# Five of eight row blocks of the mixer's output projection computed inside the attention steps, with VectorE's scaling of probabilities moved ahead of the next row maxima

## The chip, the cores and the metric

One NeuronCore of a Trainium2 chip runs the whole program: a two-layer decoder step in fp32, for one prompt of 512 tokens and 8 samples of 4 new tokens, 544 tokens in all. The metric is the device time of one execution in microseconds, the median of several runs.

## The reference

Each layer is a gated feed-forward block, a token mixer, a second feed-forward block and a small gated embedding. The change lies in the mixer, whose three branches are normalised apart, joined and projected:

```python
def _token_mixing(u, w, cache):
    z = u @ w['w_in']
    qa, ka, va, xb, gb, qc, kc, vc, oc, ic, fc = jnp.split(z, SPLIT_IDX, axis=-1)
    ...
    ya = _rms(_combine(parts).reshape(B, T, D_A).astype(u.dtype), w['g_out_a'])
    hb, hT, new_buf = _rglru(xb, conv_buf, h0, w)
    yb = _rms(jax.nn.gelu(gb) * hb.astype(u.dtype), w['g_out_b'])
    ...
    hc = jax.nn.sigmoid(oc).reshape(B, T, N_HEADS_C, DV_C) * hc.astype(u.dtype)
    yc = _rms(hc, w['g_out_c'].reshape(N_HEADS_C, DV_C)).reshape(B, T, D_C)
    y = jnp.concatenate([ya, yb, yc], axis=-1) @ w['w_out']
```

Branch A is dilated attention (384 features, 6 heads), branch B a gated linear recurrence (384), branch C a matrix memory (256). `w_out` is 1024 by 1024, so in blocks of 128 it has 8 row blocks: 3 for A, 3 for B, 2 for C.

## The kernel before

Activations lie feature-major, 128 features by 544 tokens to a tile, in two halves of 272 tokens. A precise fp32 product is made of three matmuls in the type fp32r: `block3` (L468, matmul on L473) multiplies high part by high part, high by low and low by high, for each half, so one 128 x 128 weight block costs 6 matmuls of 272 columns. Weights come in chunks of 8 blocks (512 KB). SyncE loads a chunk into one of two `raw` buffers (L392), ScalarE casts it to the high part `wh` (L922, `split`), GpSimd subtracts to get the low part `wl` (L1689, `lo_parts`), and TensorE uses it; `wh` and `wl` are rings of four chunks. A load waits until the chunk two before it has its low part (`lo`), a cast until the chunk four before it has been used (`used`). Every engine runs its own program in the order in which it is written; semaphores are the only ties.

The mixer of one layer runs in this order. First 24 tiles of the input projection, of which the last six stand between the steps of branch C's memory (`spread_g`, `qk`, `read`, `update` on TensorE, t = 0 to 3, L701), after branch B is done. Then `STEPS_A` = 15 attention steps (L828). There are 12 pairs, a pair being two heads and one block of 128 queries, with 128, 256, 384 or 512 keys by turns. In step i TensorE issues `scores(i)`, `values(i-2)` and `turn(i-1)` (transposes of the probabilities, L738), and after them, in certain steps, work for the samples against the cache: `sample_scores`, `sample_turn`, `sample_values`, `sample_out`. VectorE finds the row maxima of pair i (L1544) as soon as its scores are there, then scales the probabilities of pair i-1 by the inverse of their sums (`by_sum`, L1550), then copies the output of pair i-2 (L1599), then does its sample work. ScalarE computes the exponentials of pair i (L1088) and copies the transposed probabilities of pair i-1 out of PSUM (L1099). Scores take PSUM banks 0 and 1, the samples 2 and 3, transposes 4 and 5, and values 6 and 7 by turns. SyncE loads the key and value cache in eight groups (m = 0 to 7) of four 672 KB loads into two halves, each when TensorE has freed its half (`kv_used`). The chunks of the output projection wait: five were loaded before the attention, but the two masks for the samples lie in the ring slot of the fourth.

After the last step ScalarE squares all 8 branch tiles (L1127), TensorE sums them over the partitions (L862), ScalarE turns the four means into inverse roots (L1131, L1133), and VectorE and ScalarE make the high and low parts of the 8 normalised tiles (L1327, L1167, L1322). Only then does the output projection start: eight output tiles of 8 blocks each, the first three interleaved block by block. VectorE copies each finished tile out of PSUM (L1276), ScalarE squares it (L928) and VectorE sums the squares (L1224) for the norm that follows.

## Time and profile before

| | us |
|---|---|
| median of 3 runs | 2561.22 (2561.19 to 2565.79) |
| the profiled execution | 2555.39 |
| its span, from first to last instruction | 2553.7 |
| mean granted clock of TensorE, of full speed | 0.966 |
| TensorE matmul busy | 2395.2 (94% of the span) |
| VectorE, ScalarE, GpSimd busy | 975.2, 795.4, 872.3 |
| chain that ended last, on TensorE | 85% |

Busy shares are means over the whole span; the attention of layer 0 lies between 640 and 725 us and that of layer 1 between 1907 and 1992 us. In the stretches view the columns are the length, then TensorE's matmuls, its weight loads, VectorE, ScalarE and GpSimd, each with busy microseconds and instructions, then the granted clock of TensorE, the share of the DMA engines and GB/s. In groups and timelines PE is TensorE, DVE VectorE, ACT ScalarE, POOL GpSimd and SPq SyncE's DMA queue; a bracket tells how long the engine was idle before the row and what ended that.

### The profile page before, as it was taken

The numbers are of one execution on the slowest core, as the hardware profiler recorded it, in microseconds if no ns is written. First come the engines' busy times: TensorE is split into PE (matmuls) and PEld (weight loads), VectorE is DVE, ScalarE is ACT, GpSimd is POOL, SyncE is SP. The second block draws the span as 40 slices with busy tenths as digits, with TensorE's granted clock in tenths as the row PEclk, the third lists the DMA queues.
The fourth block names the chain that finished last, engine by engine and source line by source line (L and its number), as shares of the span: only waits on it lengthen the run. The fifth ranks groups of instructions, "written<-read, shape, count | busy, mean of one in ns | idle before, by whom it ended". The sixth has DMA issues, their size and how long they took to land.

```text
span 2553.7 us, 42609 instructions
## 1 busy us (share of the span) xinstructions
PE 2395.2 (94%) x18938; PEld 2298.0 (90%) x18938; DVE 975.2 (38%) x1363; ACT 795.4 (31%) x1141; POOL 872.3 (34%) x374
## 2 busy tenths in 40 slices
PE   6999999999788999999899999989997889999996
PEld 6999998988368999999889999989883789999996
DVE  3333303665445333202553331047554453332035
ACT  3222223331434322223442222234213442222243
POOL 3433443432013434344333344424210234434431
PEclk9999999999889999999999999999888999999998
DMA  3222232222812322332222222322128123222221
GB/s 125 98 90 88 91 98 84 83 81 70 312 62 66 107 90 83 100 99 90 70 72 90 87 85 91 100 68 91 65 89 317 62 67 99 82 90 100 93 90 52
DMA packets 72287, 247.40 MB, mean 97 GB/s; under 512 B 14296, under 2 KB 14560, under 8 KB 72160
## 3 DMA queue, kind: packets, MB, share of 16 engines
q1 hardware_dynamic: 72160, 245.59, 28.6%
q8 instruction: 95, 1.56, 0.2%
q14 instruction: 32, 0.26, 0.0%
HBM read 238.68 MB, written 6.88 MB: 96 GB/s over the span
## 4 chain that ended last, share of the span: by engine, by line
PE 85%; DVE 9%; ACT 4%; issue 1%; DMA 1%; SPq 0%; POOL 0%; DVEq 0%; ACTq 0%
PE psum L473 77%; PE psum L778 1%; DVE y_z L1673 1%; PE psum L738 1%; PE psum L812 1%; DVE x L1237 1%; DVE pp L1544 1%; PE psum L726 1%; PE psum L862 1%; DVE y_ff L1234 1%; ACT sq L928 1%; DVE xc L1361 1%; PE psum L603 1%; PE psum L637 1%; DVE z L1338 0%
## 5 line engine op out<-in xcount | busy, mean ns | idle before, releaser
L1689 POOL TENSOR_TENSOR wl<-raw,wh 128x1024 fp32r<-128x1024 f32 x356 | 863.9, 2428 | 1593.2 <-ACT wh L922 1593.1
L473 PE MATMUL psum<-xh,wh 128*128 128x272 f32 x4096 | 866.9, 293 | 83.2 <-DVE xl L1230 27.8
L473 PE MATMUL psum<-xh,wl 128*128 128x272 f32 x4096 | 857.2, 291 | 0.0
L473 PE MATMUL psum<-xl,wh 128*128 128x272 f32 x4096 | 855.2, 291 | 0.0
L473 PEld LDWEIGHTS psum<-xh,wh 128*128 128x128 f32 x4096 | 655.7, 192 | 93.2 <-DVE xl L1230 30.3
L922 ACT CAST wh<-raw 128x1024 fp32r<-128x1024 f32 x356 | 372.5, 1047 | 1133.5 <-PE psum L473 1066.1
L473 PEld LDWEIGHTS psum<-xl,wh 128*128 128x128 f32 x4096 | 654.9, 192 | 0.0
L473 PEld LDWEIGHTS psum<-xh,wl 128*128 128x128 f32 x4096 | 650.1, 192 | 0.0
L473 PE MATMUL psum<-hh,wl 128*128 128x272 f32 x1408 | 291.5, 288 | 0.0
L473 PE MATMUL psum<-hh,wh 128*128 128x272 f32 x1408 | 291.1, 288 | 0.0
L473 PE MATMUL psum<-hl,wh 128*128 128x272 f32 x1408 | 290.2, 288 | 0.0
L1267 DVE TENSOR_TENSOR hl<-act_out,hh 128x544 fp32r<-128x544 f32 x88 | 217.6, 2473 | 90.5 <-ACT hh L969 90.5
L1265 DVE TENSOR_TENSOR act_out<-act_out,psum 128x544 f32<-128x544 f32 x88 | 63.5, 721 | 415.8 <-PE psum L473 405.1
L473 PEld LDWEIGHTS psum<-hh,wh 128*128 128x128 f32 x1408 | 221.4, 188 | 0.0
L473 PEld LDWEIGHTS psum<-hl,wh 128*128 128x128 f32 x1408 | 221.3, 189 | 0.0
L473 PEld LDWEIGHTS psum<-hh,wl 128*128 128x128 f32 x1408 | 219.8, 189 | 0.0
L1274 DVE TENSOR_TENSOR y_ff<-psum,r 128x544 f32<-128x544 f32 x32 | 23.2, 725 | 448.5 <-PE psum L473 448.5
L1262 DVE TENSOR_TENSOR act_out<-psum,r 128x544 f32<-128x544 f32 x88 | 63.6, 723 | 182.0 <-PE psum L473 133.2
L928 ACT ACTIVATE sq<-y_ff 128x544 f32<-128x544 f32 x32 | 21.1, 659 | 157.5 <-DVE y_ff L1274 157.5
L1338 DVE TENSOR_TENSOR z<-psum,r 128x544 f32<-128x544 f32 x48 | 34.0, 719 | 93.2 <-PE psum L473 75.2
L947 ACT ACTIVATE xh<-x,pc 128x544 fp32r<-128x544 f32 x64 | 47.9, 748 | 48.3 <-DVE x L1237 48.3
L966 ACT ACTIVATE act_out<-act_out 128x544 f32<-128x544 f32 x88 | 57.5, 653 | 14.5 <-DVE act_out L1262 14.4
(218 smaller groups left out, 1485.5 us busy)
## 6 DMA issues: line engine op xcount, KB each, us to landing
raw<-in_weights SPq DMA_DIRECT2D x356, 512.0 KB, 3.5
kv<-in_kc SPq DMA_DIRECT2D x32, 672.0 KB, 7.8
kv<-in_vc SPq DMA_DIRECT2D x32, 672.0 KB, 6.5
x<-in_x SPq DMA_DIRECT2D x4, 544.0 KB, 7.1
out_x<-x SPq DMA_DIRECT2D x8, 272.0 KB, 2.0
mask<-in_consts SPq DMA_DIRECT2D x4, 456.0 KB, 3.8
out_v<-z SPq DMA_DIRECT2D x2, 816.0 KB, 4.3
out_k<-z SPq DMA_DIRECT2D x2, 816.0 KB, 4.4
```

The costliest lines, as they stand in the source:

```text
L473: ins = pe.matmul(T(t)[:, h, :], w, r[:, h, :], start=first and n == 0, stop=last and n == 2)
L603: ins = pe.matmul(psum[:, 2, h * P:h * P + n], ident[0:HC, h:h + 1].to_broadcast([HC, P]), gg[:, t * P:t * P + n], start=True, stop=True)
L637: ins = pe.matmul(psum[r, 5, o:o + n], w, at_[0:n, 2 * c + p, 0:n], start=True, stop=(t == 0))
L922: act.copy(wh[:, G % RING, :], raw[:, G % 2, :]).then_inc(hi.sem, 1)
L928: act.activation(sq[:, k % 2], src, ACT.Square).then_inc(sq_ready.sem, 1)
L947: act.activation(xh[:, k], x[:, k], ACT.Copy, scale=g).then_inc(nh_ready.sem, 1)
L966: act.activation(act_out[:, f % 2], act_out[:, f % 2], ACT.Silu).then_inc(silu_ready.sem, 1)
L1262: ve.tensor_tensor(act_out[:, b], T(2 * b), r2[:], ALU.mult).then_inc(gate_ready.sem, 1)
L1265: ve.tensor_tensor(act_out[:, b], act_out[:, b], T(2 * b + 1), ALU.mult).then_inc(h_ready.sem, 1)
L1267: ve.tensor_tensor(hl[:, f], act_out[:, b], hh[:, f].bitcast(F32), ALU.subtract) \
L1338: ve.tensor_tensor(two, T(t), r2[:], ALU.mult).then_inc(z_ready.sem, 1)
L1689: po.tensor_tensor(wl[:, G % RING, :], raw[:, G % 2, :], wh[:, G % RING, :].bitcast(F32), ALU.subtract).then_inc(lo.sem, 1)
```

## The change

The output projection is split by row blocks. The part for branches B and C (5 of 8 blocks) is cut into 16 fills, one for each output tile and half of the tokens; a fill is 15 matmuls into one PSUM bank, copied to SBUF. Twelve are issued in attention steps 3 to 14, ahead of `turn`, one right after the last step and three behind the sum of attention's squares. The part for branch A (3 blocks) follows attention, and VectorE adds it to the copied early part. For this, branch B is normalised within the memory steps and split into high and low parts; branch C in attention steps 0 to 2. The weights of one layer become 182 chunks instead of 178: eight of 5 blocks (`X_OB`), four of two times 3 blocks (`X_OA`) in place of eight of 8. SyncE loads chunks between the cache loads. The masks of the samples leave the weight ring, and values use PSUM bank 6 alone, fills bank 7. Apart from that, VectorE's scaling of pair i-1 moves ahead of the row maxima of pair i. The names `CH_...` become `X_...` throughout, which isn't shown.

```diff
@@ block.sync: between the cache loads, m = 0 to 7
-                load_to(CH_D2 + 5)
+                    if m == 1 or m >= 4:
+                        load_to(X_OB + (6 if m == 1 else m + 3))
+                load_to(X_D2 + 5)
...
@@ block.tensor: memory steps
                     qk(t + 1)
                     read(t)
                     update(t)
+                    if t == 1:
+                        pe.wait_ge(z_ready.sem, z_ready.at(L, E_MEM + 2))
+                        group_mean(T(0), ones, [z2[:, k] for k in range(ZXB, ZXB + 3)], 1)
+                        pe.wait_ge(gr_ready.sem, gr_ready.at(L, 1))
...
+                def fill(u, bank):
+                    d, h = u // 2, u % 2
+                    G = L * X_ALL + X_OB + d
+                    if u == 0:
+                        pe.wait_ge(nl_ready.sem, nl_ready.at(L, N_OUT * KT + B_BLOCKS))
+                    elif u <= FILL_END:
+                        pe.wait_ge(fill_ready.sem, fill_ready.at(L, u))
+                    if h == 0:
+                        pe.wait_ge(lo.sem, G + 1)
+                    for n, (k, l, m) in enumerate(EARLY):
+                        w_h, w_l = (v[:, G % RING, n * P:(n + 1) * P] for v in (wh, wl))
+                        for o, (w, r) in enumerate(((w_h, zr[:, m, h, :]), (w_h, zr[:, l, h, :]), (w_l, zr[:, m, h, :]))):
+                            ins = pe.matmul(psum[:, bank, 0:HALF], w, r, start=n == 0 and o == 0,
+                                            stop=n == B_BLOCKS - 1 and o == 2)
+                    ins.then_inc((used if h else fill_done).sem, 1)
...
@@ block.tensor: values
-                    if j >= 2:
-                        pe.wait_ge(o_ready.sem, o_ready.at(L, j - 1))
+                    if j:
+                        pe.wait_ge(o_ready.sem, o_ready.at(L, j))
...
-                            ins = pe.matmul(psum[r, 6 + j % 2, 0:P], vt[:, kb, h * HD:(h + 1) * HD],
+                            ins = pe.matmul(psum[r, 6, 0:P], vt[:, kb, h * HD:(h + 1) * HD],
...
@@ block.tensor: attention steps and what follows
+                    if i == 1:
+                        pe.wait_ge(tm_ready.sem, tm_ready.at(L, 11))
+                        for c, t in enumerate((T(1), T(3))):
+                            group_mean(t, blk, [z2[:, ZQC + c]], 4 + c)
+                    if i == 2:
+                        pe.wait_ge(gr_ready.sem, gr_ready.at(L, 3))
                     if 2 <= i < PAIRS + 2:
                         values(i - 2)
+                    if i >= FILL_STEP:
+                        fill(i - FILL_STEP, 7)
                     if 1 <= i < PAIRS + 1:
                         turn(i - 1)
...
+                fill(FILL_END, 7)
+                group_mean(T(0), ones, [xh_sq[:, k] for k in range(3)], 6)
+                for u in range(FILL_END + 1, 2 * KT):
+                    fill(u, 7 - (u - FILL_END))
+                pe.wait_ge(gr_ready.sem, gr_ready.at(L, 4))
...
@@ block.scalar: memory steps
+                    if t == 2:
+                        for n in range(3):
+                            early_hi(L, n)
                     split(G + E_MEM + t + RING)
+                    if t == 0:
+                        act.wait_ge(b_done.sem, b_done.at(L, 1))
+                        for k in range(3):
+                            act.activation(z2[:, ZXB + k], z2[:, ZGB + k], ACT.Square).then_inc(gs_ready.sem, 1)
+                    if t == 1:
+                        group_rstd(L, 1, acc[:], T(0), DB)
...
@@ block.scalar: ahead of and in the attention steps
+                split(G + 3)
+                act.wait_ge(c_done.sem, c_done.at(L, 1))
+                for c in range(2):
+                    act.activation(z2[:, ZQC + c], z2[:, ZVC + c], ACT.Square).then_inc(gs_ready.sem, 1)
...
+                    if i == 1:
+                        for c in range(2):
+                            group_rstd(L, 2 + c, z2[:, ZOC + c], T(1 + 2 * c), HD)
+                    if i == 2:
+                        for c in range(2):
+                            early_hi(L, 3 + c)
+                    if i >= FILL_STEP:
...
+                        act.copy(Y_OUT[d][:, h, :], psum[:, 7, 0:HALF]).then_inc(fill_ready.sem, 1)
+                        if h and d < 5:
+                            split(G + d + RING)
...
@@ block.vector: late projection
+            def out_a(L):
+                for d in range(KT):
...
+                    ve.tensor_tensor(Y_OUT[d], Y_OUT[d], T(d % 4), ALU.add).then_inc(y_ready.sem, 1)
+                    if 1 <= d < KT - 1:
+                        add_square(L, 1, d)
...
@@ block.vector: memory steps
+                    if t == 2:
+                        ve.wait_ge(gr_ready.sem, gr_ready.at(L, 1))
+                        for n in range(3):
+                            early_normed(L, n, acc[:])
+                    if t == 3:
+                        for n in range(3):
+                            early_lo(L, n)
                     z_tile(L, E_MEM + t)
...
@@ block.vector: attention steps; the same lines are taken out behind the row maxima
                 for i in range(STEPS_A):
+                    if 1 <= i < PAIRS + 1:
+                        pair = (2 * i - 2, 2 * i - 1)
+                        n = ((i - 1) % 4 + 1) * P
+                        for u in pair:
+                            ve.wait_ge(e_ready.sem, e_ready.at(L, u + 1))
+                            ve.reciprocal(stat[:, u % 4, 3:4], stat[:, u % 4, 2:3]).then_inc(ri_ready.sem, 1)
+                        for u in pair:
+                            ve.wait_ge(ri_ready.sem, ri_ready.at(L, u + 1))
+                            by_sum(stat[:, u % 4], pp[:, u % 4, 0:n]).then_inc(p_done.sem, 1)
...
+                        ve.wait_ge(gr_ready.sem, gr_ready.at(L, 3))
+                        for c in range(2):
+                            early_normed(L, 3 + c, z2[:, ZOC + c])
+                    if i == 2:
+                        for c in range(2):
+                            early_lo(L, 3 + c)
```

`early_normed` is one `scalar_tensor_tensor` on a tile, `early_hi` ScalarE's cast of it to the high part, `early_lo` VectorE's subtraction; `group_mean` is two matmuls for each tile of squares, `group_rstd` an Ln and an Exp.

## Rows read from the trace of the kernel before

**Rows 1.** Stretches view: length, then busy us (instructions) by engine, granted clock, DMA.

```profile
554.00:612.00 58.00, 57.35 (x462) 49.82 (x461) 22.13 (x41) 13.09 (x29) 16.96 (x12) 0.94 0.22 75
...
640.00:725.10 85.10, 61.72 (x574) 33.14 (x573) 37.13 (x167) 31.53 (x91) 0.00 (x0) 0.86 0.70 267
```

**Rows 2.** Chain that ended last: start us, us, what.

```profile
50.68 373.10 PE psum L473 x2976
...
738.57 50.00 PE psum L473 x384
```

**Rows 3.** Groups view, attention stretch, TensorE: busy us, mean ns | idle before.

```profile
L738 PE MATMUL psum<-con,pp 128*128 128x128 f32 x60 | 11.4, 331 | 17.4 <-DVE pp L1550 17.4
```

**Rows 4.** Timeline, TensorE, attention steps: start us, us, instructions [idle before].

```profile
648.78 0.66 PE L738 MATMUL psum<-con,pp 128*128 128x128 f32 x2 [3.40 <-DVE pp L1550]
...
652.95 1.12 PE L738 MATMUL psum<-con,pp 128*128 128x128 f32 x4 [1.31 <-DVE pp L1550]
...
654.31 3.98 PE L778 MATMUL psum<-kv,qbd 128*32 128x456 f32 x24 [0.25 <-DMA kv<-in_kc]
...
722.52 0.55 PE L825 MATMUL psum<-con,so 128*128 128x128 f32 x3 [0.68 <-DVE so L1629]
```

**Rows 5.** Chain that ended last, in the recurrent branch.

```profile
489.45 0.92 PE psum L566 x4
```

**Rows 6.** Timeline of ScalarE, attention steps and group norm.

```profile
644.50 0.83 ACT L1080 COPY vs<-psum 16x384 f32<-16x384 f32 x2
...
660.95 0.72 ACT L1088 ACTIVATE pp<-pp,stat 128x512 f32<-128x512 f32 x1 [6.47 <-DVE stat L1547]
...
668.06 0.39 ACT L1088 ACTIVATE pp<-pp,stat 128x128 f32<-128x128 f32 x1
...
669.06 1.07 ACT L1099 COPY ptp<-psum 128x512 f32<-128x512 f32 x2
...
724.29 4.48 ACT L1127 ACTIVATE y_ff<-z 128x544 f32<-128x544 f32 x8 [8.63 <-DVE z L1611]
...
730.46 0.66 ACT L1133 ACTIVATE gr<-gr 128x544 f32<-128x544 f32 x1
```

**Rows 7.** Timelines of VectorE and ScalarE, late in the output projection.

```profile
767.12 2.47 DVE L1224 TENSOR_TENSOR acc<-acc,sq 128x544 f32<-128x544 f32 x1 [1.20 <-ACT sq L928]
...
777.89 1.04 ACT L922 CAST wh<-raw 128x1024 fp32r<-128x1024 f32 x1
...
778.02 0.73 DVE L1224 TENSOR_TENSOR acc<-acc,sq 128x544 f32<-128x544 f32 x1 [0.73 <-ACT sq L928]
...
788.60 0.72 DVE L1276 COPY y_z<-psum 128x544 f32<-128x544 f32 x1 [3.84 <-PE psum L473]
```

**Rows 8.** Timeline of VectorE, attention steps.

```profile
667.77 0.88 DVE L1550 TENSOR_SCALAR pp<-pp,stat 128x512 f32<-128x512 f32 x2
...
723.11 1.10 DVE L1611 COPY z<-psum 64x16 f32<-64x16 f32 x6 [0.64 <-PE psum L825]
```

**Rows 9.** Stretches view, two pieces of the attention steps.

```profile
704.00:708.00 4.00, 2.32 (x19) 1.30 (x20) 3.08 (x12) 1.45 (x5) 0.00 (x0) 1.00 0.75 255
...
712.00:716.00 4.00, 4.00 (x32) 2.74 (x32) 0.29 (x1) 1.49 (x4) 0.00 (x0) 0.57 0.06 20
```

**Rows 10.** Timelines of VectorE and GpSimd, memory steps.

```profile
594.04 0.42 DVE L1473 TENSOR_TENSOR kw<-kc,wt 128x256 f32<-128x256 f32 x1
...
604.73 2.40 POOL L1689 TENSOR_TENSOR wl<-raw,wh 128x1024 fp32r<-128x1024 f32 x1 [8.26 <-ACT wh L922]
...
605.56 1.84 DVE L1473 TENSOR_TENSOR kw<-kc,wt 128x256 f32<-128x256 f32 x1
```

**Rows 11.** Timeline of TensorE, first matmuls of the output projection.

```profile
740.84 0.66 PE L473 MATMUL psum<-xh,wh 128*128 128x272 f32 x2
...
741.29 0.66 PE L473 MATMUL psum<-xl,wh 128*128 128x272 f32 x2
```

**Rows 12.** DMA issues: out<-in, count, KB each, us from issue to landing.

```profile
kv<-in_kc SPq DMA_DIRECT2D x32, 672.0 KB, 7.8
```

More of the change, by code:

```diff
@@ L239, in build @@
         quarters = lambda v: v.rearrange("p (q n) -> p q n", q=4)
+        Y_FF, Y_Z = ([v[:, k] for k in range(KT)] for v in (y_ff, y_z))
+        Y_OUT = [xl_y[:, k] for k in range(3)] + [z2[:, k] for k in Y_TILES]
         def column(L, c):
@@ L592, in turn_v, with group_mean @@
                     ins.then_inc(tm_done.sem, 1)
+                def group_mean(t, over, squares, first):
+                    for k, sq_k in enumerate(squares):
+                        pe.wait_ge(gs_ready.sem, gs_ready.at(L, first + k))
+                        for h in range(2):
+                            ins = pe.matmul(t[:, h, :], over, sq_k[:, h, :], start=(k == 0),
+                                            stop=(k == len(squares) - 1))
+                    ins.then_inc(gst_done.sem, 1)
                 def z_tile(e, t):
@@ L881, in _ @@
                 mix_tensor(pe, L)
-                first_tiles(L, N_OUT, G + CH_OUT)
-                for d in range(4, KT):
-                    pe.wait_ge(y_ready.sem, y_ready.at(L, KT + d - 3))
-                    tile(d % 4, G + CH_OUT + d)
+                out_a(L)
                 y_mean_square(L, 1)
```

343 lines of the change are left out of this document (207 added, 136 removed).

## The prediction

> **What bounds the kernel now.** I read the stretches view first. Between 554 and 612 us, where the last input-projection tiles run between the memory branch's steps, TensorE is busy 57.35 of 58.00 us; in layer 0's attention steps, 640 to 725 us, it is busy only 61.72 of 85.10 us, and GpSimd does nothing at all [rows 1]. The chain of waits shows what follows: TensorE's L473 carries the chain nearly everywhere, at 373.10 us for 2976 matmuls (0.1254 us each), and the output projection is 384 of them, 50.00 us, that begin only at 738.57, when attention is over [rows 2]. The groups view of the attention stretch names the idle time: 17.4 us stand before the transposes of the probabilities (`turn`, L738), ended by VectorE's scaling L1550 [rows 3]. The timeline says how they are spread: 3.40 and 1.31 us before the first two, so 17.4 - 4.7 = 12.7 us before those of steps 3 to 11, and 0.68 us more before the last `sample_out` [rows 4]. That 13.4 us per layer is the hole; 5 of the 8 row blocks of the projection need no attention result and can fill it. Layer 1 repeats the pattern, so I work out layer 0 and double it.
>
> **Part 1, the recurrent branch's norm goes into the memory steps.** TensorE is full there [rows 1], so what it gains in work or waits is on the path. At t = 1 it issues 6 matmuls of 272 columns against `ones` and then waits for `gr_ready`. Four fp32 matmuls of that shape took 0.92 us [rows 5], so 6 take 1.4. The wait is ScalarE's Ln and Exp, 0.66 us each by the Exp's row, with two handoffs 1.5 [rows 6]. Queued behind it on TensorE are `spread_g(3)` and tile E_MEM+2; VectorE and GpSimd then wait for these. Sum **+2.9 us** (1.4 if the Exp were hidden, 5 if a square came late). ScalarE's three squares and three hi copies, and VectorE's three scalings and three subtractions, fall into engines that are busy for under half of this stretch: 22.13 and 13.09 of 58 us [rows 1]. They cost nothing while each stays ahead of the next tile; uncovered, the three scalings would be some 2.3 us, by the 0.72 of another VectorE operation on a tile of that size [rows 7].
>
> **Part 2, the start of attention.** The memory branch's group norm stands in steps 0 to 2. I walk the chain from the last token-major copy on ScalarE, which ends at 644.50 + 0.83 = 645.3 [rows 6]. New before the first exponential: a chunk cast of 640 columns (640/1024 of 1.04 us [rows 7] = 0.65) and two squares (4.48/8 each [rows 6], 1.2 with handoff), to 647.2. Two exponentials of 128 columns, at 0.39 us each, take it to 648.0 [rows 6]. Scaling of pair 0 and the row maxima of pair 1 on VectorE, some 1.6 (an estimate; the scaling alone of two 512-column rows is 0.88 [rows 8]), to 649.6; exponentials of pair 1 at 256 columns, 1.0, between the rows of 128 and 512 columns [rows 6]; two Ln/Exp pairs, 2 x 1.3, to 653.2, while TensorE waits for `gr_ready` at step 2 and VectorE behind its own wait for it; two normalisations, 1.5; the scaling of pair 1, 0.8, to 655.5. The second `turn` began at 652.95 before [rows 4]: **+2.5 us** (1 to 5). The first cache keys hide almost none of it, since they held TensorE for only 0.25 us [rows 4].
>
> **Part 3, twelve fills in steps 3 to 14.** A fill is 15 matmuls of 272 columns, 15 x 0.1254 = 1.88 us; twelve are 22.6. They stand ahead of `turn`, in the very holes of [rows 3, 4], which give back 13.4. The scaling that VectorE now issues ahead of the next row maxima needs the exponentials (2 x 0.72 us at 512 columns [rows 6]) and then 0.88 us [rows 8]; with scores, values and a fill TensorE has 3 to 4 us of its own before it asks, so `turn` no longer waits. By the same count the old VectorE order would also be ready in time once a fill stands there, so I cost the reordering by itself at 0 +- 1 us per layer; the wait it would remove without fills is the one the fill covers. A new wait: on ScalarE the copy of pair i-1's transposed probabilities comes after exponentials i, the evacuation of the fill (about 0.4, less than one of the two 512-column copies that make 1.07 [rows 6]) and on every second step a 0.65 us cast. Step 4, counted from its start: the sample's maxima and scaling 3 hold the row maxima back to 3.3 us, so exponentials end at 4.1, the evacuation at 4.5, the cast at 5.2, the copies at 6.3, while TensorE comes to `values(3)` at 4.9: it waits 1.5 us there, and by the same walk 0.4 in step 7: +1.9. Elsewhere sample work on TensorE covers it. That fills and values now have one PSUM bank each costs nothing, because a whole step lies between the use of a bank and its next one; without that step each fill would wait the 0.4 us of its evacuation. Between 712 and 716 us the granted clock was 0.57, so at the lower of its two levels (1.2 of 2.4 GHz) for most of that time, with TensorE busy throughout and attention work behind it [rows 9]; at the upper level those 4 us are 2.3. With the holes filled I take 2.5 us back for the whole stretch, whose mean clock was 0.86 [rows 1] (0 to 4). Sum 22.6 - 13.4 + 1.9 - 2.5 = **+8.6 us** (5 to 13). SyncE's queue now has a chunk load behind the cache loads m = 1 and 4 to 7; each waits for GpSimd's `lo` two chunks earlier, done by my walk over 10 us before the next cache half is freed: 0.
>
> **Part 4, the end.** Before: the last sample copy ends at 723.11 + 1.10 = 724.2 [rows 8] and the last tile's evacuation at 788.60 + 0.72 = 789.3 [rows 7], 65.1 us. After, from the same point: three squares (2.05), 6 matmuls of the mean (1.4), three fills (5.7): the late projection starts at 9.4. The Ln, Exp, scale, hi, lo chain beside it (1.3 for the first two and 0.7 for each of the rest, after the mean at 3.6 [rows 6, 7]) gives its first operand at 7 to 8. Late work is 144 matmuls, 18.1 us, so TensorE alone would end at 28.3 with one evacuation. But a tile now takes TensorE 18 x 0.1254 = 2.26 us where it took 6, and VectorE needs per tile an add of 0.72, a wait of 0.73 for ScalarE's square and 0.73 for the sum: 2.18 [rows 7]. The first three tiles run interleaved, the first ends at 9.4 + 5.3 = 14.7, and from there VectorE needs 0.75 + 6 x 2.18 + 0.75 = 14.6 us; one sum beside a GpSimd subtraction costs 2.47 for 0.73 [rows 7], +1.7. End at 31.0: VectorE, not TensorE, sets it. **-34.1 us** (-28.9 with four such collisions, -36.8 at TensorE's pace).
>
> **The sum.** 2.9 + 2.5 + 8.6 - 34.1 = -20.1 us per layer, -40.2 in two. Against the profiled execution, 2555.39 us of which the span is 2553.7, that is 2515.2; its time lies 5.8 under the median of the runs, 2561.22, from which I get **2521**.
>
> **A rule that speaks against it.** GpSimd, idle in the attention steps [rows 1], now subtracts six chunks there. Near 605 us VectorE's L1473 took 1.84 us and ended just after GpSimd's L1689, against 0.42 with GpSimd idle [rows 10]. The Trainium skill, "SBUF — State Buffer", "Who interferes with whom", calls the port pair of the two engines an exclusive lock, in which the later one blocks for the whole instruction, VectorE's `tensor_scalar` in a two-port mode included; these rows agree for an operation with two inputs, and none shows it for the scaling L1550. By it each of the six could hold a scaling.
>
> **The rivals.** (a) GpSimd holds VectorE: six times 1.84 - 0.42 = 1.42 us, all on the path, is +8.5 per layer, -23 in all: 2538. For: [rows 10]. Against: a subtraction follows a cast, which follows the evacuation of a fill, and most scalings are over by then. (b) ScalarE's queue becomes the bound: the 1.5 us stall of step 5 in all twelve steps is 18 - 1.9 = +16.1 per layer: 2553. Against: ScalarE is busy 31.53 of 85.10 us [rows 1], and in seven steps sample work stands between. (c) The granted clock stays at the lower level: pairs of L473 matmuls then stand 0.45 us apart, 0.225 each [rows 11], so 180 of them cost 18 more, with the 2.5 not regained +20.4 per layer: 2562, no change. Against: from 704 to 708 us the clock was 1.00 with TensorE busy for only 2.32 of 4.00 us [rows 9]. (d) Slower: the chunk loads in SyncE's queue hold the cache loads behind them until TensorE needs them. A load takes 7.8 us to land [rows 12]; four of them unhidden are +31 per layer, more than the 20.1 won: -40.2 + 62 gives 2583. It decides from where `lo` of the earlier chunk comes later than TensorE's release of the cache half. Against: the 10 us of part 3.
>
> **How the numbers follow.** Forecast 0.70, by itself 2508 to 2534 from the bounds of parts 1 to 4; (a) 0.10, (b) 0.10, (c) 0.05, (d) 0.05. The range must leave out no more than 0.2, so it takes in (a) and not (b) to (d): 2508 to 2541. A measurement of this kernel can tell about 0.2%, 5 us, from no change. Forecast, (a) and (b) are faster by more: 0.90. (c) is the same: 0.05. (d) is slower: 0.05.
>
> **What would show it.** In the changed profile: L738's idle time should fall from 17.4 to under 4 us per layer; the stretch from the end of the first sample scores (step 2) to the last sample copy should grow by about 8.6 us; ScalarE's Exp should end a TensorE wait of about 1.5 us in the memory steps; VectorE's adds, not TensorE, should end the late projection, about 31 us after the last sample copy. The prediction is wrong if VectorE operations in the attention steps lengthen beside GpSimd (a), if `values` waits for the copies of ScalarE in most steps (b), if the granted clock there is near 0.5 (c), or if TensorE waits for cache loads (d).

## The result and the profile after

| | before | after |
|---|---|---|
| median of the runs, us | 2561.2 | 2528.4 |
| profiled execution, us | 2555.39 | 2529.01 |
| its span, us | 2553.7 | 2527.3 |

The change makes the kernel faster: the ratio after to before is 0.987, 95% interval 0.9852 to 0.9888, so 32.8 us. I forecast 2521 us, 40.2 less, in a range of 2508 to 2541: the sign, the place and most of the size are right. The two profiled spans differ by only 26.4 us, because work outside the change took 7.4 us longer in the profiled execution of after: the 578.3 us ahead of the third memory step are the same work in both kernels, and took 582.1 after, at a granted clock of 0.98 instead of 0.99; the work behind the mixer of layer 1 took 501.0 us at 0.97 instead of 497.4 at 0.98 (stretches view of both). So below I measure each kernel over **the changed stretch** of a layer, from the start of the gate rows of memory step 2 (`spread_g(2)`) to the end of VectorE's last evacuation or add of the mixer's output: 211.0 and 212.3 us before, 194.9 and 194.8 after, -16.1 and -17.5, so 33.6 us in all.

Stretches view of after, layer 0: attention from the end of the first sample scores to the last sample copy, from there to the late projection, and the late projection (length, then busy us and instructions of TensorE, its weight loads, VectorE, ScalarE, GpSimd, the granted clock, DMA share, GB/s).

```profile
671.60:743.70 72.10, 67.68 (x692) 47.28 (x688) 27.36 (x125) 29.58 (x83) 8.02 (x5) 1.00 0.68 256
...
743.70:754.10 10.40, 10.30 (x72) 9.86 (x73) 4.46 (x9) 5.79 (x10) 1.81 (x1) 1.00 0.12 39
...
754.10:777.00 22.90, 18.84 (x147) 18.52 (x146) 14.19 (x17) 8.81 (x12) 10.78 (x5) 0.94 0.32 94
```

The same attention stretch before, and the groups of TensorE in it, before and then after (busy us, mean ns, idle time in front and what ended it):

```profile
658.30:724.20 65.90, 49.09 (x508) 26.33 (x508) 28.15 (x129) 22.95 (x66) 0.00 (x0) 0.92 0.67 257
```

```profile
L738 PE MATMUL psum<-con,pp 128*128 128x128 f32 x54 | 9.7, 319 | 12.7 <-DVE pp L1550 12.7
```

```profile
L815 PE MATMUL psum<-ptp,vt 128*64 128x128 f32 x116 | 8.8, 282 | 1.2 <-ACT ptp L1237 1.2
...
L803 PE MATMUL psum<-con,pp 128*128 128x128 f32 x54 | 7.5, 272 | 0.0
```

Where TensorE was busy for 49.09 of 65.90 us of this stretch (61.72 of 85.10 over the longer one of [rows 1]), it is now busy for 67.68 of 72.10. The 12.7 us in front of the transposes (of the 17.4 in [rows 3]) are gone, and the mean clock of the stretch went from 0.92 to 1.00. Timeline of TensorE in after: the mean of the recurrent branch, the wait behind it, the wait of `values(3)`, the closing mean, the start of the late projection.

```profile
593.53 2.91 PE L635 MATMUL psum<-z,con 128*128 128x272 f32 x12
...
597.84 1.15 PE L648 MATMUL psum<-gg,con 4*128 4x128 f32 x8 [1.40 <-ACT acc L1089]
...
684.66 1.09 PE L815 MATMUL psum<-ptp,vt 128*64 128x128 f32 x16 [0.99 <-ACT ptp L1237]
...
745.75 2.91 PE L635 MATMUL psum<-xh_sq,con 128*128 128x272 f32 x12
...
754.14 0.41 PE L510 MATMUL psum<-xh,wh 128*128 128x272 f32 x2
```

By stage, from the same points in the timelines of both kernels, measured as after for before:

| stage | forecast | layer 0 | layer 1 |
|---|---|---|---|
| 1, `spread_g(2)` to the first sample update of the memory | +2.9 | 60.1 for 52.8, +7.2 | 60.0 for 55.7, +4.3 |
| 2, first scores to the end of the first sample scores | +2.5 | 19.9 for 17.6, +2.4 | 19.9 for 18.4, +1.5 |
| 3, from there to the last sample copy | +8.6 | 72.1 for 65.9, +6.1 | 72.1 for 64.0, +8.1 |
| 4, from there to the last evacuation or add | -34.1 | 33.3 for 65.1, -31.8 | 33.3 for 64.9, -31.6 |
| sum | -20.1 | -16.1 | -17.5 |

From the sample updates to the first scores nothing is changed (9.6 us after; 9.6 and 9.3 before, and the sum of layer 1 holds the difference). After is the same in both layers, before is not: its memory steps behind `spread_g(4)`, TensorE busy throughout, took 29.8 us at a clock of 0.94 in layer 0 and 32.7 us at 0.84 in layer 1 (31.3 at 0.89 after, in both). That stretch is the same work for TensorE in all kernels, so what it adds to stage 1, +1.5 in layer 0 and -1.4 in layer 1, is the clock's.

### The profile page after: what moved, and what is told of

Same layout as the page of the kernel before. It is cut to its first block, busy times and chain, and to the rows that moved or that the text cites. A ratio compares the mean times of both kernels' runs of the same rounds, so it can differ in the third digit from the quotient of the medians.

```text
span 2527.3 us, 42699 instructions
## 1 busy us (share of the span) xinstructions
PE 2392.1 (95%) x18938; PEld 2300.2 (91%) x18938; DVE 966.2 (38%) x1371; ACT 800.9 (32%) x1173; POOL 871.8 (34%) x382
## 4 chain that ended last, share of the span: by engine, by line
PE 86%; DVE 8%; ACT 5%; issue 1%; DMA 0%; POOL 0%; SPq 0%; DVEq 0%; ACTq 0%
PE psum L510 75%; PE psum L780 2%; DVE acc L1358 1%; PE psum L843 1%; DVE y_z L1848 1%; ACT sq L1019 1%; PE psum L877 1%; DVE x L1371 1%; DVE y_ff L1368 1%; PE psum L648 1%; PE psum L815 1%; PE psum L682 1%; PE psum L791 0%; DVE gt L1531 0%; DVE z L1477 0%
## 5 line engine op out<-in xcount | busy, mean ns | idle before, releaser
L1865 POOL TENSOR_TENSOR wl<-raw,wh 128x1024 fp32r<-128x1024 f32 (+2 forms) x364 | 862.5, 2371 | 1562.5 <-ACT wh L1013 1562.5
L510 PE MATMUL psum<-xh,wh 128*128 128x272 f32 x3936 | 835.2, 294 | 73.6 <-DVE xl L1364 26.7
L510 PE MATMUL psum<-xh,wl 128*128 128x272 f32 x3936 | 825.6, 292 | 0.0
L510 PE MATMUL psum<-xl,wh 128*128 128x272 f32 x3936 | 823.6, 291 | 0.0
L1013 ACT CAST wh<-raw 128x1024 fp32r<-128x1024 f32 (+2 forms) x364 | 373.8, 1028 | 1136.7 <-PE psum L510 1070.0
L510 PEld LDWEIGHTS psum<-xh,wh 128*128 128x128 f32 x3936 | 632.4, 192 | 83.3 <-DVE xl L1364 29.9
L510 PEld LDWEIGHTS psum<-xl,wh 128*128 128x128 f32 x3936 | 631.5, 192 | 0.0
L510 PEld LDWEIGHTS psum<-xh,wl 128*128 128x128 f32 x3936 | 626.4, 192 | 0.0
L510 PE MATMUL psum<-hh,wl 128*128 128x272 f32 x1408 | 291.4, 288 | 0.0
L510 PE MATMUL psum<-hh,wh 128*128 128x272 f32 x1408 | 291.1, 288 | 0.0
L510 PE MATMUL psum<-hl,wh 128*128 128x272 f32 x1408 | 290.2, 288 | 0.0
L510 PEld LDWEIGHTS psum<-hh,wh 128*128 128x128 f32 x1408 | 221.4, 188 | 0.0
L510 PEld LDWEIGHTS psum<-hl,wh 128*128 128x128 f32 x1408 | 221.3, 189 | 0.0
L510 PEld LDWEIGHTS psum<-hh,wl 128*128 128x128 f32 x1408 | 219.7, 189 | 0.0
L1396 DVE TENSOR_TENSOR act_out<-psum,r 128x544 f32<-128x544 f32 x88 | 63.6, 723 | 182.3 <-PE psum L510 133.2
L1019 ACT ACTIVATE sq<-y_ff 128x544 f32<-128x544 f32 x32 | 21.1, 658 | 157.5 <-DVE y_ff L1407 157.5
L780 PE MATMUL psum<-z_split,wh 128*128 128x272 f32 x320 | 64.3, 297 | 2.5 <-DVE z L1763 2.5
```

The lines of the kernel that those rows point to most:

```text
L510: ins = pe.matmul(T(t)[:, h, :], w, r[:, h, :], start=first and n == 0, stop=last and n == 2)
L780: ins = pe.matmul(psum[:, bank, 0:HALF], w, r, start=n == 0 and o == 0, stop=n == B_BLOCKS - 1 and o == 2)
L1013: act.copy(wh[:, G % RING, 0:n], raw[:, G % 2, 0:n]).then_inc(hi.sem, 1)
L1019: act.activation(sq[:, k % 2], src, ACT.Square).then_inc(sq_ready.sem, 1)
L1396: ve.tensor_tensor(act_out[:, b], T(2 * b), r2[:], ALU.mult).then_inc(gate_ready.sem, 1)
L1865: po.tensor_tensor(wl[:, G % RING, 0:n], raw[:, G % 2, 0:n], wh[:, G % RING, 0:n].bitcast(F32), ALU.subtract).then_inc(lo.sem, 1)
```

## The experiments

A run of one kernel against another can differ by some microseconds because the clock falls to its lower level at other places: the kernel before alone lay between 2554.4 and 2569.2 us on one chip. So every experiment is read by its median and by its changed stretches. The edits are shown shortened, in words where the code is long.

| kernel | median, us | ratio to before, 95% | changed stretch, layer 0 and 1 |
|---|---|---|---|
| before | 2561 to 2567 | | 211.0, 212.3 |
| order alone | 2538.1 | 0.9867 to 0.9909 | 202.1, 202.1 |
| old order | 2528.0 | 0.9834 to 0.9871 | 194.7, 194.7 |
| after | 2528.4 | 0.9852 to 0.9888 | 194.9, 194.8 |
| short fills | 2501.7 | 0.9735 to 0.9781 | 185.5, 182.3 |
| add first | 2520.1 | 0.9810 to 0.9846 | 188.2, 191.0 |
| small lo | 2518.7 | 0.9798 to 0.9852 | 192.1, 191.5 |
| late wait | 2521.9 | 0.9812 to 0.9857 | 192.9, 192.7 |
| mean in fp32r | 2513.4 | 0.9781 to 0.9827 | 188.0, 189.4 |
| fill first | 2528.5 | 0.9831 to 0.9877 | 194.8, 194.8 |
| combined | 2509.9 | 0.9767 to 0.9822 | 184.4, 184.2 |

### Old order: the change without VectorE's reordering

```diff
-    by_sum of pair i-1
     row_max and exp_bias of pair i
+    by_sum of pair i-1
```

> The changed kernel with one part undone: VectorE takes the row maxima of pair i first and scales the probabilities of pair i-1 behind them, as in the kernel before (in step 1 still ahead of its wait for the group statistics). The fills stay. Prediction's theory: with a fill of 1.9 us ahead of each turn the scaling is ready in time in either order, so the order alone is worth 0 +- 1 us per layer: 2526 to 2531 us, and the turn (L803) stays without idle time of note. Rival: the order carries the gain, and the waits of 1.41 us ahead of nine turns per layer come back beside the fills: 2 x 12.7 = 25 us more, 2554 us.

Measured: 2528.04 us, changed stretches 194.7 and 194.7 where the changed kernel has 194.9 and 194.8. Stretches and groups view of the attention:

```profile
671.20:742.60 71.40, 67.43 (x689) 47.07 (x688) 28.20 (x129) 29.35 (x83) 8.03 (x5) 1.00 0.69 259
```

```profile
L815 PE MATMUL psum<-ptp,vt 128*64 128x128 f32 x116 | 8.8, 282 | 0.7 <-ACT ptp L1237 0.7
...
L803 PE MATMUL psum<-con,pp 128*128 128x128 f32 x54 | 7.5, 272 | 0.0
```

TensorE is busy for 67.43 of 71.40 us, and no idle time stands in front of `turn` (L803) here either. With the fills in place the order is worth nothing that can be measured, as forecast.

### Order alone: the kernel before with nothing but the reordering

```diff
     for i in range(STEPS_A):
+        by_sum of pair i-1
         row_max and exp_bias of pair i
-        by_sum of pair i-1
```

> The kernel before with the order alone: VectorE scales the probabilities of pair i-1 ahead of the row maxima of pair i; no fills, and the output projection as before. Theory A: the idle time of TensorE ahead of the turns (12.7 us per layer in steps 3 to 11) was the scaling's place behind the row maxima, and goes: up to 25 us less, 2536 us. Theory B (the one behind the 0 +- 1 of the prediction): the row maxima, two exponentials, the reciprocals and the scalings of one pair follow each other on VectorE and ScalarE, so scaling first holds the next row maxima back by what it brings the turn forward; the wait moves from the turn to the scores or the next step: 2556 to 2566 us, and the stretch from the end of the first sample scores to the last sample copy stays at 64 to 67 us (65.9 before).

Measured: 2538.12 us against 2566.95 of before on the same chip, so 28.8 less by the medians, 16.5 less by the spans of the two profiled executions (before's profile is near its fastest run), and 8.9 and 10.3 us less in the changed stretches. Theory A holds in the main, theory B falls.

```profile
664.20:718.50 54.30, 44.91 (x512) 24.35 (x508) 27.03 (x125) 22.34 (x66) 0.00 (x0) 0.99 0.80 309
```

```profile
L738 PE MATMUL psum<-con,pp 128*128 128x128 f32 x54 | 8.1, 283 | 2.2 <-DVE pp L1550 2.2
```

The idle time in front of the transposes went from 12.7 to 2.2 us and the attention stretch from 65.9 to 54.3, without one matmul of the projection in it (in layer 1 from 64.0 to 57.1). Not all of the wait is won: all idle time of the stretch fell from 16.8 to 9.4 us, because TensorE now waits 1.8 us for ScalarE's copies and 0.7 us for a cache load (2.5 us in layer 1), where before waited 0.1 us at most; the other 4.2 us of the 11.6 are the same matmuls at a higher clock, 0.99 for 0.92. The changed stretches differ from these numbers by up to 3.4 us, mostly by the memory steps behind `spread_g(4)`, which took 32.7 and 29.8 us here for 29.8 and 32.7. Together with the last run these are all four combinations. The order is worth 9 to 10 us per layer without fills (11.6 and 6.9 by the attention stretch alone) and nothing with them; the fills with what belongs to them are worth 16 to 18 us per layer without the order, and 7.2 on top of it. Both edits close the same hole.

### Short fills: what the twelve fills cost where they stand

```diff
     for n, (k, l, m) in enumerate(EARLY):
+        if n and u < FILL_END: continue
         for o, (w, r) in enumerate(...):
+            if o and u < FILL_END: continue
```

> The changed kernel with the twelve fills of the attention steps cut from 15 matmuls to 1 each, so that 14/15 of the early projection of six of the eight output tiles is not computed; every wait, evacuation, cast and chunk load stays. What is taken away is 12 x 14 x 0.1254 = 21.1 us of TensorE per layer. Prediction's theory: 13.4 us of the fills lie in holes, so the stretch from the first sample scores to the last sample copy (72.1 us in the changed kernel) shrinks by only 7 to 9 us per layer, to 63 to 65 us: 2511 to 2515 us. Rival 1: nothing is hidden and TensorE is the bound throughout: 21 us per layer, 51 us of stretch, 2486 us. Rival 2: ScalarE's and VectorE's chain sets the steps even with the fills, and nothing is gained: 2528 us.

Measured: 2501.68 us, 26.7 less than the changed kernel; the attention stretch is 60.5 us, 11.6 less (in layer 1, at a clock of 1.00, 58.0 us, 14.1 less).

```profile
668.10:728.60 60.50, 50.23 (x524) 27.24 (x520) 27.91 (x130) 29.39 (x83) 8.01 (x5) 0.94 0.79 307
```

```profile
L819 PE MATMUL psum<-ptp,vt 128*64 128x128 f32 x116 | 8.8, 282 | 3.8 <-ACT ptp L1241 3.7
...
L807 PE MATMUL psum<-con,pp 128*128 128x128 f32 x54 | 7.7, 275 | 1.2 <-DVE pp L1700 1.2
```

None of the three forecasts has it: of the 21.1 us of matmuls taken out of each layer, 13.4 were on the path by the medians (26.7 / 2), 9.4 and 12.5 by the changed stretches. That is more than the 7 to 9 I gave, because with VectorE's new order the 13.4 us of holes are no longer there for the fills to use (`order_alone` has 2.2 us left in front of `turn`). Without the fills TensorE is idle for 10.3 of the 60.5 us, most of it for ScalarE's copies of the transposed probabilities (L819, 3.8 us), and only 1.2 us of it for the scaling (L807).

### Add first: does VectorE set the late projection?

```diff
     ve.tensor_tensor(Y_OUT[d], Y_OUT[d], T(d % 4), ALU.add)
-    if 1 <= d < KT - 1:
-        add_square(L, 1, d)
+    if d >= 2:
+        add_square(L, 1, d - 1)
```

> The changed kernel with one change in the late projection: VectorE adds tile d+1 before it sums the square of tile d, so its wait for ScalarE's square lies beside an add. Prediction's theory (VectorE, not TensorE, sets the end): the last add ends at TensorE's pace, 144 x 0.1254 = 18.1 us and one add of 0.71 behind the start of the late projection, so 19 us where it takes 22.8 (754.14 to 776.98): 4 us less per layer, 2520 us. Rival: the three sums that take 1.8 to 1.9 us beside GpSimd's subtractions are the bound by themselves, and adds that now stand beside GpSimd lengthen too: at most 1 us per layer is won, 2526 to 2528 us.

Measured: 2520.05 us; from its start to the last add the late projection takes 18.96 us (750.69 to 769.65) where after takes 22.84: 3.9 less in each layer, as the theory has it. Chain of waits, then VectorE's and GpSimd's timelines:

```profile
753.99 14.92 PE psum L510 x119
```

```profile
760.56 1.77 DVE L1358 TENSOR_TENSOR acc<-acc,sq 128x544 f32<-128x544 f32 x1
...
762.25 0.71 DVE L1417 TENSOR_TENSOR z<-z,psum 128x544 f32<-128x544 f32 x1
...
762.88 2.45 DVE L1358 TENSOR_TENSOR acc<-acc,sq 128x544 f32<-128x544 f32 x1
...
768.93 0.72 DVE L1417 TENSOR_TENSOR z<-z,psum 128x544 f32<-128x544 f32 x1 [0.89 <-PE psum L510]
...
759.34 2.41 POOL L1865 TENSOR_TENSOR wl<-raw,wh 128x1024 fp32r<-128x1024 f32 x1 [4.33 <-ACT wh L1013]
...
762.35 2.39 POOL L1865 TENSOR_TENSOR wl<-raw,wh 128x1024 fp32r<-128x1024 f32 x1 [0.61 <-ACT wh L1013]
...
767.67 2.60 POOL L1865 TENSOR_TENSOR wl<-raw,wh 128x1024 fp32r<-128x1024 f32 x1 [2.92 <-ACT wh L1013]
```

TensorE's L510 now carries the chain through the whole of it (the view begins at 754; the matmuls begin at 750.69). Two sums beside GpSimd's subtractions still take 1.77 and 2.45 us, but VectorE has caught up by the last add, which waits 0.89 us for TensorE. The rest of the 6.6 us in layer 0's changed stretch is the clock in the memory steps, 41.3 us for 44.3 from `spread_g(3)` to the first sample update.

### Small lo: what makes three of the sums long?

```diff
-    n = width(G)
+    n = 8 if X_F2 <= G % X_ALL < X_F2 + 3 else width(G)
```

> The changed kernel with GpSimd's low-part subtraction of the three weight chunks that fall beside the late projection cut from 1024 columns to 8, so that the low parts of the first three chunks of the second feed-forward are not computed. Theory: VectorE's sums of squares (1.88, 1.89, 1.83 us) are long because GpSimd's subtraction runs beside them; they fall to 0.72, and since VectorE sets the end of the late projection, 3 x 1.15 = 3.5 us per layer go: 2521 us. Rival 1: they are long for another reason (ScalarE's cast and square run then too) and stay at 1.8: 2528 us. Rival 2: they shorten, but the late projection does not, because TensorE or ScalarE then ends it: 2526 to 2528 us.

Measured: 2518.69 us; the late projection takes 19.4 us in both layers, 3.4 less. VectorE's timeline in after, GpSimd's beside it, and VectorE's with the subtractions cut:

```profile
763.88 1.88 DVE L1358 TENSOR_TENSOR acc<-acc,sq 128x544 f32<-128x544 f32 x1 [0.73 <-ACT sq L1019]
...
767.12 0.72 DVE L1358 TENSOR_TENSOR acc<-acc,sq 128x544 f32<-128x544 f32 x1 [0.73 <-ACT sq L1019]
...
769.20 1.89 DVE L1358 TENSOR_TENSOR acc<-acc,sq 128x544 f32<-128x544 f32 x1 [0.72 <-ACT sq L1019]
...
762.78 2.40 POOL L1865 TENSOR_TENSOR wl<-raw,wh 128x1024 fp32r<-128x1024 f32 x1 [4.33 <-ACT wh L1013]
...
768.10 2.40 POOL L1865 TENSOR_TENSOR wl<-raw,wh 128x1024 fp32r<-128x1024 f32 x1 [2.92 <-ACT wh L1013]
```

```profile
760.59 0.73 DVE L1358 TENSOR_TENSOR acc<-acc,sq 128x544 f32<-128x544 f32 x1 [0.73 <-ACT sq L1019]
...
764.75 0.73 DVE L1358 TENSOR_TENSOR acc<-acc,sq 128x544 f32<-128x544 f32 x1 [0.73 <-ACT sq L1019]
```

A sum takes 1.88 and 1.89 us while a subtraction of GpSimd runs and 0.72 when none does; with the subtractions gone every sum takes 0.73. So the cause of the length is GpSimd, and its price is that of the theory, 3 x 1.15. Both long sums end 0.6 us behind the end of the subtraction (765.76 for 765.18, 771.09 for 770.50), so what a sum pays depends on how much of the subtraction is left when it starts.

### Late wait: the pause in the memory steps

```diff
     spread_g(t + 1)
+    if t == 2: pe.wait_ge(gr_ready.sem, gr_ready.at(L, 1))
     z_tile(E_MEM + t, 0)
     ...
         group_mean(T(0), ones, ...)
-        pe.wait_ge(gr_ready.sem, gr_ready.at(L, 1))
```

> The changed kernel with the wait for the recurrent branch's group statistics moved: TensorE takes the next step's gate rows (spread_g(3)) first and waits only ahead of the next input-projection tile, whose PSUM tile the statistics are read from. Theory A: only the wait shortens, from 1.15 us to near 0.3: 0.9 us per layer, 2526 us. Theory B: the pause also brings the granted clock to its lower level behind it (0.57 from 600 to 604 us), so with a shorter pause those 4 us run at 1.00 and another 1.5 us per layer come back: 2523 to 2524 us. Against both: the rest of the wait appears ahead of the tile: 2528 us.

Measured: 2521.86 us, but the changed stretches are only 2.0 and 2.1 us shorter; the other 2.4 us lie in work that is the same in both kernels (`spread_g(2)` starts at 579.89 for 582.10, for one). The wait is 0.32 us where it was 1.40 in the row of the wait above:

```profile
595.63 0.52 PE L510 MATMUL psum<-xh,wh 128*128 128x272 f32 x2 [0.32 <-ACT acc L1090]
```

Stretches of 4 us, after and then late wait (length, TensorE's busy us, granted clock):

```profile
598.00:602.00 4.00, 4.00 (x26) 0.80 0.01 4
...
630.00:634.00 4.00, 4.00 (x88) 0.64 0.23 82
...
634.00:638.00 4.00, 4.00 (x26) 0.51 0.02 4
```

```profile
598.00:602.00 4.00, 4.00 (x34) 1.00 0.00 0
...
626.00:630.00 4.00, 4.00 (x71) 0.50 0.28 82
...
630.00:634.00 4.00, 4.00 (x20) 0.50 0.01 4
...
634.00:638.00 4.00, 4.00 (x27) 0.77 0.00 0
```

Theory B's clock did come back, to 1.00, in the 4 us behind the wait. From `spread_g(2)` to `spread_g(4)` TensorE takes 26.2 us for 28.8 in both layers: 1.1 us of the wait and 1.5 of the clock. The other runs agree. Seven kernels have the wait of 1.40 us, and the step behind it took 13.0 to 13.1 us in 13 of their 14 layers (11.5 in layer 0 of `add_first`), in `mean_r` too, where the mean ahead of the wait is short. Without the wait the step took 11.5 (before, `order_alone`), and 11.9 with 0.32 of wait in it (here and `combined`).

The second dip, 626 to 638, is not the first one moved. In every kernel the clock is 1.00 from `spread_g(4)` up to the samples' part of `read` (L695 in after), whose matmuls have four columns, and falls while these run or just behind them: in after 32 of them took 1.10 us at 628.18 and 1.87 at 632.57. How long that dip lasts differs: the stretch behind `spread_g(4)` took 29.8 to 32.7 us over all kernels, and before alone took both. Here it took 32.7 in both layers for 31.3 in after, so 1.5 of the 2.6 us are lost again; in `combined`, which has the same short wait, it took 31.3. The other 0.9 us of the changed stretch lie in unchanged stages up to the last sample copy.

### Mean in fp32r: what a group mean costs

```diff
-    pe.matmul(t, ones, z2 squares (fp32))
+    pe.matmul(t, ones_r, zr squares (fp32r))
```

> The changed kernel with the squares and the ones of the two 384-row group means (memory steps and end of attention) held as fp32r instead of fp32, so that one matmul is one pass. Theory: a mean of six fp32 matmuls shows as 12 records and 2.77 us, 0.46 us per matmul of 272 columns, where an fp32r matmul of that width takes 0.1254; six then take 0.75 us, so 2.0 us less at each of two places per layer, both on the path: 8 us, 2520 us. Rival: the two records are how the profile writes a matmul, and the 2.77 us are the clock's lower level or the loading of the weights: nothing changes, 2528 us. Between: the mean at the end is hidden by the three fills behind it, 2524 us.

Measured: 2513.39 us, 15.0 less; the changed stretches are 6.9 and 5.4 shorter. Timeline of TensorE, with the wait behind the mean:

```profile
594.52 0.99 PE L640 MATMUL psum<-z_split,ones_r 128*128 128x272 f32 x6
...
596.91 1.15 PE L653 MATMUL psum<-gg,con 4*128 4x128 f32 x8 [1.40 <-ACT acc L1094]
```

Six records and 0.99 us stand where twelve and 2.91 stood. At the two places themselves the gain is 2.0 us each (`spread_g(2)` to `spread_g(3)` 13.7 for 15.7, last sample copy to late projection 8.4 for 10.4), 4.0 per layer, as the theory has it; what goes beyond that is the clock's (1.4 us in each layer in the memory steps behind `spread_g(4)`, 29.8 for 31.3).

### Fill first: the fill ahead of the values

```diff
-    if 2 <= i < PAIRS + 2: values(i - 2)
     if i >= FILL_STEP: fill(i - FILL_STEP, 7)
+    if 2 <= i < PAIRS + 2: values(i - 2)
```

> The changed kernel with each fill ahead of the values of its step instead of behind them. Theory: the values wait for ScalarE's copies of the transposed probabilities (0.99 us in step 5, 0.16 in step 7, 0.85 for the sample's), and a fill of 1.9 us ahead of them covers that: 1.1 to 2 us less per layer, 2524 to 2526 us. Rival: the attention output then leaves PSUM 1.9 us later and ScalarE's copies wait for the values, so the wait moves to the turn: 2528 to 2532 us.

Measured: 2528.46 us, stretches 194.8 and 194.8: nothing. The waits of `values` are gone, and up to the sample's transposes of step 5 it is 0.6 us ahead, but in step 11 that is lost. Timeline of VectorE and TensorE there, fill first and then after:

```profile
724.00 0.29 DVE L1751 COPY z<-psum 128x128 f32<-128x128 f32 x1 [0.87 <-PE psum L815]
...
725.12 1.10 DVE L1763 COPY z<-psum 64x16 f32<-64x16 f32 x6 [0.83 <-PE psum L890]
...
726.37 1.06 PE L860 MATMUL psum<-con,psm 128*128 128x128 f32 x8 [1.28 <-DVE z L1763]
```

```profile
723.45 0.28 DVE L1751 COPY z<-psum 128x128 f32<-128x128 f32 x1
...
725.40 1.10 DVE L1763 COPY z<-psum 64x16 f32<-64x16 f32 x6 [1.67 <-PE psum L890]
...
726.64 1.06 PE L860 MATMUL psum<-con,psm 128*128 128x128 f32 x8 [1.28 <-DVE z L1763]
```

VectorE's copy of the attention output now waits 0.87 us for the values, and the sample copy, for which TensorE waits 1.28 us in both kernels, stands behind it. Counted from the end of the first sample scores TensorE goes on at the same time in both (726.37 - 671.39 = 726.64 - 671.64 = 55.0). The rival named the cause, the late values, but not the place.

### Combined: a version that beats both

```diff
     late projection: add(d+1) ahead of the sum of square d
     means: fp32r squares and ones
     memory steps: wait behind spread_g(3)
-    wait for the last copies; fill(12); mean; fill(13..15)
+    fill(12); wait for the last copies; fill(13); mean; fill(14), fill(15)
```

> The changed kernel with four edits together: the add of tile d+1 ahead of the sum of tile d's square in the late projection; the 384-row means in fp32r; the wait for the recurrent branch's statistics behind the next step's gate rows; and two of the last four fills ahead of the closing mean instead of one, the first of them ahead of the wait for the last sample copy. Theory: their stages add up, because TensorE is the bound in each of them once the edit is made. Per layer 3.9 us (late projection, 22.8 to 18.9), 4.0 us (two means), 1.1 us (wait) and 1.5 us (closing fills: last sample copy to late projection 10.4 to 6.9 with the mean's 2.0), 10.5 us in all, so 21 us in two layers: 2507 us, with 3 to 4 us either way for where the clock's lower level falls. Rival: with the mean short and the fills ahead, the late projection waits for its operand (square, mean, Ln, Exp, scale, high part, low part: 8.8 us from the last sample copy in the changed kernel, 6.8 with the short mean), so that the closing fills give nothing: 2510 us.

Measured: 2509.94 us, ratio 0.9794 [0.9767, 0.9822] to before, so faster than before. It is also 18.4 us below the median of after, which was measured at another time; the slowest of its runs, 2510.2, lies below the fastest of after, 2526.2. The changed stretches are 184.4 and 184.2, 10.5 and 10.6 less than after, the sum that was forecast, but its terms are not, so the sum came by luck. In layer 0, from `spread_g(2)` to `spread_g(4)`, it is 4.6 us (28.8 to 24.2) for the 3.1 of mean and wait: the clock behind the wait, 1.5, was left out. Last sample copy to late projection is 2.7 (10.4 to 7.7) for 3.5, the late projection 2.5 (22.8 to 20.4) for 3.9, and 0.6 lies in unchanged stages. The two short terms have their reason in the rows:

```profile
738.13 0.51 PE L786 MATMUL psum<-z_split,wh 128*128 128x272 f32 x2
...
741.98 0.92 PE L640 MATMUL psum<-xh_sq,ones_r 128*128 128x272 f32 x6
...
746.85 0.49 PE L512 MATMUL psum<-xh,wh 128*128 128x272 f32 x2 [0.19 <-issue]
...
749.11 0.43 DVE L1798 COPY z<-psum 128x272 f32<-128x272 f32 x1
...
749.68 0.49 PE L512 MATMUL psum<-xh,wh 128*128 128x272 f32 x2 [1.10 <-DVE z L1798]
```

The first of the four closing fills now starts at 738.13, right behind the transposes of the sample's output, so of the 8.7 us to 746.85 four fills are 7.5, the mean 0.75 and idle time 0.19: TensorE is full. What is won is that it starts 1.0 us ahead of the end of the last sample copy (739.12), less some tenths: 0.7 us, where I had 1.5 because I counted a whole fill as hidden. In the late projection TensorE waits 1.10 us at 749.68, which neither after nor `add_first` does. The third output tile waits there for VectorE to copy the last fill out of PSUM, and in VectorE's order that copy stands behind the normalisations and low parts of branch A, which wait for the closing mean. This is most of the 1.4 us by which the late projection is longer than in `add_first` (20.4 for 19.0); sums beside GpSimd's subtractions do not explain it, since they are as long there. So the closing fills win 0.7 us and lose more than that behind it. The rival, who had them give nothing, was right about them, though TensorE waits for a copy and not for its operand.

## Why the prediction was right, and where it was not

**What bounds the kernel.** Right. TensorE had a hole of 12.7 + 0.7 us per layer in attention, work of the projection went into it, and the idle time in front of `turn` fell from 17.4 to 1.2 us in the whole of attention (under 4 was forecast; the 1.2 stand in front of the second transposes).

**Part 1, +2.9: too low, by a term that was mis-sized and one that was left out.** The mean was costed at 1.4 us for six matmuls, from [rows 5], read as four matmuls in 0.92 us. The rows count records, and an fp32 matmul leaves two: the six came as 12 records, 2.91 us by the row above and 2.77 us in the chain of waits, where overlaps are left out (0.46 us each), and the rows I had used were two matmuls, not four. The wait, 1.40 us, was forecast at 1.5. So the step from `spread_g(2)` to `spread_g(3)` is 15.7 us for 11.5, +4.2. The next step is 1.5 us longer, 13.1 us at a clock of 0.87 where before had 11.5 at 1.00, and I had no term for that; `late_wait` shows that it follows the wait. The step after that, 31.3 us, is longer than before's in layer 0 and shorter in layer 1, so it says nothing of the change. `mean_r` and `late_wait` measure what the two terms can give back: 2.0 us and about 1.1, with 1.5 of the clock behind the wait. ScalarE's Exp does end the wait, as I said it would. The Trainium skill, "FP8 and Floating Point Precision", "TensorE Precision Notes", gives a true fp32 product four passes through the array; by that, four times the 0.1254 us of an fp32r matmul is an estimate of 0.50 us, near the 0.46 measured.

**Part 2, +2.5: right**, +2.4 and +1.5 in the two layers. In layer 0 the chain is the one that I walked; at the second `turn`, where the walk ends, it is +1.95 (14.17 us behind the first scores for 12.22), and the rest is the first sample scores, 4.71 us for 3.98.

**Part 3, +8.6: 2.5 too high in layer 0 and 0.5 in layer 1, each term a little off.** In layer 0 TensorE's busy time grew by 18.6 us (49.09 to 67.68), of which the fills are 22.6, so the clock gave back 4.0 and not 2.5 (2.8 in layer 1, where before's clock was 0.95). The idle time fell from 16.8 to 4.4 us, 12.4, where 13.4 less 1.9 of new stalls were forecast. Those stalls came where the walk had them, but smaller: 0.99 us in front of `values(3)`, forecast 1.5, and 0.16 in step 7, forecast 0.4. ScalarE is behind it in that order: evacuation, cast, copies. Chunk loads in SyncE's queue held nothing up: no wait of TensorE for a cache load is in the attention stretch of after.

**The reordering, 0 +- 1: right beside the fills, and the sentence about it was the better half.** I wrote that the wait which the order would remove without fills is the one that the fill covers; `order_alone` and `old_order` show exactly that. What I left out is what follows: the kernel before needed none of the projection moved to win half of the changed stretch's gain (9 to 10 of 16 to 18 us). Of the fills' 22.6 us only 5.0 lie in idle time once the order is there (idle 9.4 us in `order_alone`, 4.4 after), and the other 17.6 lengthen attention (54.3 to 72.1). They pay because the end loses 31.8 us.

**Part 4, -34.1: right in mechanism, 2.3 short.** VectorE does end the late projection (its adds and sums, with ScalarE's squares between, carry the chain, and `add_first` moves the end to TensorE's pace), 33.3 us behind the last sample copy, not 31.0: the mean at 2.75 us and not 1.4, and three sums beside GpSimd at 1.83 to 1.89 us where one was in the forecast (3.5 us for 1.7); of these 3.1 us 0.8 came back elsewhere (0.25 of it because the forecast's own 2.05, 1.4 and 5.7 make 9.15 and not 9.4). The bound of four collisions had held that open.

**The sum and the range.** -16.1 and -17.5 for -20.1, and 2528.4 lies in the range. The misses are the mean, costed too low at both of its places (1.4 us each), the clock behind the wait and the collisions with GpSimd, in part made good by Part 3. The bounds of the four parts, added as they stand, give -29.4 to -5.9 per layer, so 2502 to 2549 us; the narrower 2508 to 2534 is not worked out in the prediction.

**The rivals.** (a) did not come: VectorE's scalings in attention take a median of 378 ns (384 before), but the rows leave open whether they could: no scaling ran beside a subtraction, as the text against (a) said. (b) came in two steps of twelve, as the forecast had it. (c): the clock was 1.00. (d): no wait for the cache.

**What stays open.** The clock falls at the same two places of the memory steps in nearly every kernel, but for how long differs from kernel to kernel and from layer to layer in unchanged work, and I know no rule for it from these runs. Such shifts are why the two profiled spans differ by 26.4 us and the changed stretches by 33.6, and what makes `late_wait` and `mean_r` look better by the medians than by their own stages.

## What to carry to other kernels

When two edits are aimed at one idle time, price each of them alone and both together: a hole can be given away once, and here the cheap edit (moving one VectorE instruction ahead of another) had taken most of it before any matmul was moved. Work moved into a stretch that is full costs its whole length there, so look for its gain at the place that it leaves. Compare the same stretch in every layer before a difference is put down to the change: here unchanged memory steps moved by up to 2.9 us. And count instructions in the code, not records in the trace, before a row's time is divided.

## What the runs showed of the hardware

- A 128x128 by 272-column matmul takes 0.46 us with fp32 operands, in two records, and 0.1254 us with fp32r ones (both at a granted clock of 1.00).
- VectorE's `tensor_tensor` with both inputs in SBUF takes 1.8 to 2.5 us beside a GpSimd subtraction and 0.72 without; the long ones end 0.6 us behind the subtraction. The same instruction with one input in PSUM does not lengthen: the add at 768.93 in `add_first` took 0.72 us with GpSimd's subtraction (767.67 to 770.27) running throughout. The Trainium skill, "SBUF — State Buffer", "Who interferes with whom", has both: an instruction with two SBUF inputs contends with GpSimd's reads, one with at most one SBUF input, outside the two-port modes, does not.
- The granted clock of the attention stretch in layer 0 was 0.92 before, 1.00 after and 0.99 with the order alone, where TensorE is idle for 9.4 of 54.3 us. With the short fills it was 0.94 in layer 0 and 1.00 in layer 1, with TensorE idle for 10.3 and 10.4 us. So the amount of idle time alone does not set it.
- Behind a wait of 1.40 us in an otherwise full stretch, TensorE's clock fell (0.87 over the next 13.1 us, for 1.00 over 11.5) in 13 of 14 cases (two layers of seven kernels); with the wait at 0.32 us it did not, in 4 of 4.
- The clock also fell with TensorE busy throughout: at or just behind 128 matmuls of four columns, in both layers of every kernel (in after 0.73 over these matmuls, 1.00 ahead of them).
